# Down weights of experts 3 to 15 asked for by ScalarE instead of SyncE

## The reference, cut to what matters

```python
def _expert_choice_ffn(u, w_router, w_g, w_u, w_d):
    b, n, _ = u.shape
    cap = CAPACITY_FACTOR * n // N_EXPERTS
    logits = jnp.einsum('bnd,de->ben', u, w_router, preferred_element_type=jnp.float32)
    aff = jax.nn.softmax(logits, axis=1)
    gate, idx = lax.top_k(aff, cap)
    bidx = jnp.arange(b)[:, None, None]
    xe = u[bidx, idx]
    hg = jnp.einsum('becd,edf->becf', xe, w_g)
    hu = jnp.einsum('becd,edf->becf', xe, w_u)
    ye = jnp.einsum('becf,efd->becd', jax.nn.silu(hg) * hu, w_d) * gate[..., None].astype(u.dtype)
    return jnp.zeros_like(u).at[bidx, idx].add(ye)
```

## Time and profile before

| | |
|---|---|
| median of 3 runs | 2314.52 us (2312.52 to 2320.67) |
| profiled execution, its time | 2317.68 us |
| profiled execution, its span | 2315.9 us |
| PE busy | 2015.6 us (87%) |
| ACT busy | 541.9 us (23%) |
| DVE busy | 1118.0 us (48%) |
| queue q1, SyncE's (hardware_dynamic): bytes | 737.33 MB |
| queue q0, GpSimd's (software_dynamic): bytes | 19.00 MB |
| queue q10, ScalarE's (hardware_dynamic): bytes | 0.13 MB |
| mean granted TensorE clock | 0.969 |

### The profile page before, as it was taken

How to read it: one execution, slowest core, us unless ns; L and a number is a source line. 1 busy time by engine, 2 the same in 40 slices (tenths; PEclk the granted TensorE clock), 3 DMA queues, 4 the chain that set the end, 5 groups by cost and what they waited for, 6 DMA issues and landing times.

```text
span 2315.9 us, 34904 instructions
## 1 busy us (share of the span) xinstructions
PE 2015.6 (87%) x13636; PEld 1379.1 (60%) x13636; DVE 1118.0 (48%) x1731; ACT 541.9 (23%) x838; POOL 71.6 (3%) x109
## 2 busy tenths in 40 slices
PE   7999999999999999999999986666679998666665
PEld 5999556999899845799886542222239753222222
DVE  3877777878877777887743211000017421100001
ACT  3333133433433223333423100000004210000001
POOL 0000000000000000000300000000000000000000
PEclk9999999999999999999999999999999999899988
DMA  9987876988689777788763899999998699999997
GB/s 347 334 295 261 314 255 214 294 311 302 226 286 322 253 292 255 232 308 313 251 246 104 352 419 421 422 422 422 422 408 281 259 394 421 421 422 422 422 422 317
DMA packets 240449, 757.58 MB, mean 327 GB/s; under 512 B 14016, under 2 KB 124256, under 8 KB 193136
## 3 DMA queue, kind: packets, MB, share of 16 engines
q1 hardware_dynamic: 233248, 737.33, 83.2%
q0 software_dynamic: 6864, 19.00, 2.6%
q10 hardware_dynamic: 256, 0.13, 0.0%
HBM read 755.22 MB, written 1.18 MB: 327 GB/s over the span
## 4 chain that ended last, share of the span: by engine, by line
PE 57%; DMA 32%; DVE 4%; SPq 3%; ACT 1%; issue 1%; DVEq 1%; ACTq 0%
DMA W<-in_w_exp_down 29%; PE psum L870 22%; PE psum L882 10%; PE psum L944 5%; PE psum L925 4%; PE psum L1412 3%; PE psum L1343 2%; SPq L592 2%; PE psum L1150 1%; PE psum L1302 1%; DMA W<-in_w_exp_up 1%; PE psum L787 1%; DMA W<-in_w_conv_in 1%; DMA W_mod<-in_mod_w 1%; PE psum L1324 1%
## 5 line engine op out<-in xcount | busy, mean ns | idle before, releaser
L870 PEld LDWEIGHTS psum<-parts 128*128 128x128 f32 x4224 | 517.8, 192 | 9.1 <-issue 1.9
L870 PE MATMUL psum<-parts 128*128 128x256 f32 x4224 | 521.1, 283 | 1.1 <-ACT parts L1448 0.8
L1302 PE MATMUL psum<-W,scr 128*32 128x512 f32 x1920 | 270.4, 687 | 165.6 <-DMA W<-in_w_exp_up 165.6
L1800 DVE SCALAR_TENSOR_TENSOR mod_acc<-W_mod,cond,mod_acc 128x1024 f32<-128x1024 f32 x196 | 251.8, 1285 | 45.0 <-issue 27.5
L2356 DVE TENSOR_TENSOR scr<-scr,psum 128x256 f32<-128x256 f32 x32 | 13.5, 422 | 530.5 <-ACT scr L1716 530.5
L882 PE MATMUL psum<-parts 128*128 128x512 f32 x1056 | 258.0, 393 | 0.2 <-DVE parts L1995 0.2
L1969 DVE TENSOR_TENSOR parts<-W,parts 128x1024 fp32r<-128x1024 f32 x176 | 207.2, 1220 | 70.2 <-ACT parts L1504 70.1
L1302 PEld LDWEIGHTS psum<-W,scr 128*32 128x32 f32 x1920 | 58.6, 117 | 305.3 <-issue 177.1
L882 PEld LDWEIGHTS psum<-parts 128*128 128x128 f32 x1056 | 192.5, 188 | 45.8 <-DVE parts L1982 7.8
L787 PE MATMUL psum<-k_ones,k_ident 128*128 128x256 f32 x736 | 206.2, 413 | 0.0
L787 PEld LDWEIGHTS psum<-k_ones,k_ident 128*128 128x128 f32 x736 | 135.0, 199 | 103.1 <-issue 89.7
(11 more groups left out here) (329 smaller groups left out, 1700.1 us busy)
## 6 DMA issues: line engine op xcount, KB each, us to landing
W<-in_w_exp_down SPq DMA_DIRECT2D x128, 1024.0 KB, 26.5
W_mod<-in_mod_w SPq DMA_DIRECT2D x123, 1024.0 KB, 6.5
W<-in_w_exp_up SPq DMA_DIRECT2D x120, 1024.0 KB, 26.3
W<-in_w_exp_gate SPq DMA_DIRECT2D x120, 1024.0 KB, 24.9
W<-in_ffn_w_gate SPq DMA_DIRECT2D x44, 1024.0 KB, 9.1
W<-in_ffn_w_up SPq DMA_DIRECT2D x44, 1024.0 KB, 11.6
W<-in_ffn_w_down SPq DMA_DIRECT2D x44, 1024.0 KB, 10.4
W<-in_w_in SPq DMA_DIRECT2D x24, 1024.0 KB, 8.6
```

The costliest lines, as they stand in the source:

```text
L870: ins = pe.matmul(psum[:, 4 + t % 2, S * g:S * g + S], w[:, t % 2, g, kc, :], u[:, kc, :], start=(n == 0 and kc == 0), stop=(n == 2 and kc ...
L1302: ins = pe.matmul(psum[32 * q:32 * q + 32, 4, :].rearrange("p (g n) -> p g n", g=2), x, w[:, :, q, :], start=(b == 0), stop=(b == KC - 1), ...
L1800: ins = dve.scalar_tensor_tensor(acc[:, :], w, col, acc[:, :], mul, add)
```

## The change

The 13 x 4 down blocks of experts 3 to 15, in each of the two layers, are no longer asked for in SyncE's loop. ScalarE asks for them through its own queue, in a new function `down_blocks`, called ahead of the silu of the same expert. The waits are the same ones (d0 to d3 of expert e-1), the source, slot and landing semaphore too.

```diff
--- before.py
+++ after.py
@@ -631,8 +631,6 @@
                 with sp.Fori(3, EXPERTS) as e:
                     for pair in range(4):
                         ring_blocks(layer, e, pair, 2 * pair + 1, e + (E0 - 1))
-                    for q in range(4):
-                        ring_down(layer, e, q, e + (E0 - 1))
 
             def m2_done(name):
                 return m2_pe.s, m2_pe.at(name)
@@ -1725,6 +1723,12 @@
                     act.activation(xeT[:, kc, SOME:512], psum[:, LATE_BANKS[kc % 2], 0:512 - SOME], copy, bias=u_shift[:, kc:kc + 1],
                                    scale=u_scale[:, kc:kc + 1]).then_inc(r_act.sig(f"c{kc}"), 1)
 
+                def down_blocks(e):
+                    for q in range(4):
+                        act.wait_ge(e_pe.s, e_pe.at(f"d{q}", e + (EXPERTS * layer - 1)))
+                        act.dma_start(part(W[:, KC + q, :], 0, 2, D), A["w_exp_down"][layer, ds(e, 1), 256 * q:256 * q + 256, :]
+                                      .rearrange("a (p k) n -> p (a k) n", k=2)).then_inc(landed[KC + q], 16)
+
                 def hidden_out(E):
                     act.wait_ge(e_pe.s, e_pe.at("hT", E))
                     act.activation(e_hT[:, :, :], part(psum[:, 5, :], 0, 4, P)[:, 0:2, :], copy).then_inc(e_act.sig("hT"), 1)
@@ -1737,12 +1741,14 @@
                 hidden_out(EXPERTS * layer + 1)
                 silu(EXPERTS * layer + 2)
                 hidden_out(EXPERTS * layer + 2)
+                down_blocks(3)
                 silu(EXPERTS * layer + 3)
                 for kc in (0, 2, 4, 6):
                     late_out(kc)
                 hidden_out(EXPERTS * layer + 3)
                 with act.Fori(4, EXPERTS) as e:
                     E = e + EXPERTS * layer
+                    down_blocks(e)
                     silu(E)
                     hidden_out(E)
                 roots_next()
```

## The result

The changed kernel takes 2334.1 us (median of 5 runs, 2330.97 to 2337.07), the kernel before 2319.38 us in the 5 runs taken by then (2312.52 to 2324.18). The ratio is 1.0076, 95% interval 1.0057 to 1.0094: slower by about 17 us by the ratio (the two medians lie 14.7 us apart). I had forecast slower by 10.7 us (a ratio of 1.0046) and a range of 2314 to 2333.5. The way was right, the size was too small, and the time lies just outside the range; that the kernel before came out at 2319 and not at 2314.5 in the longer series has a part in the latter.

A forecast was written before the change was run, and what follows sets the result against it. Expert stretches were taken as bound by bytes, so only the order of landing mattered: tails of 7.9 us in layer 1 and 2.8 in layer 0 sum to 10.7, and 2314.5 + 10.7 = 2325.2 us; range 2314 to 2333.5.

The forecast's parts named there:

- The steady stretch: Experts 4 to 15 of either layer: same 12 blocks per period, 29.8 us at 422 GB/s, nothing gained or lost.
- Requests: 104 requests moved from SyncE to ScalarE: cost nothing on both sides, covered by ScalarE's idle time.
- The order of landing: With two queues served in equal turns, the fourth pair's block lands last instead of a down block.
- The tail of 10.6 us: Behind layer 1's last byte: 3.87 us to the first down matmul, 4.4 us of down blocks, 2.3 us to the norm.
- The cover in layer 0: End of layer 0: the square already waited behind the third convolution block's rounding, so only +2.8 us is lost.
- Rival C: Both queues served in the order of asking, blocks land as before: no change, 2314.5 us; chance 0.08.
- D: Two queues cost bytes per us in the expert stretches: 3.5 to 7 us, 2329 to 2332; chance 0.10.
- E: Faster: SyncE's stalls gone, better filled queues move more bytes, each 1% giving 7 us; chance 0.06.
- Rival B: ScalarE's queue gets a third of the turns, fourth down block lands last: about +5.5 us, 2320; chance 0.14.
- Then the queues take turns: Within one expert's period: from 5 us, 4 down and 4 gate or up blocks take 19.9 us, to 24.9.
- The clock term: Each layer's tail: TensorE waits ahead of the third pair, reads it slowly, so the fourth starts 0.7 us late.
- The start costs nothing: At experts 3 and 4, the queues do not run empty, with a margin of 4 us; cost nothing.

The follow-up runs named there:

- experts 6 to 14: Against the kernel before, ScalarE asks for the down blocks of experts 6 to 14 only, SyncE for those of 3 to 5 and 15; ratio 0.9998.
- the run with 8 unread matmuls: Changed kernel with 12 instead of 2 unread matmuls ahead of the third pair, 8 instead of 2 ahead of the fourth; ratio 1.0057 to the kernel before.
- The run that has the start but not the end: Changed kernel with expert 15's four down blocks asked for by SyncE again, in both layers; ratio 1.0023 to the kernel before.

## Why the prediction was short

**Right, by its own steps.** The steady stretch gives and takes nothing (422 GB/s, and 0.9998 for experts 6 to 14). Requests cost nothing that can be seen, on either engine. The second queue isn't served behind the first, and the turns are equal: down blocks land 5.0 us apart. The order of landing changes, the last wait is for an up block, and the loss stands behind it: moving the last expert alone brings most of it, moving it back takes most of it away. The tail of 10.6 us without the clock was right to the tenth in the two traces with a fast fourth pair. The cover in layer 0 was real and is now shown by two runs. Rival C (landing in the order of asking) and D (a lower rate) are excluded by the traces, E by the ratio. Rival B (a third of the turns) had the last wait on a down block and would have them land 7.5 us apart; the last wait was for an up block, and they land 5.0 us apart.

**The step that failed.** "The down slots are free at about 5 ... Then the queues take turns ... to 24.9" lets the turns begin with the request. In the changed kernel the first down block of a group landed 9.0 us after its request, where two turns take 5.0: the turns began about 4 us late. The requests came later too where the fourth pair was read slowly: 7.9 us after the start of that read (2279.59 to 2287.51), not 5. So the eight shared turns reached to the end of the period, the fourth pair landed inside them and not behind them, and it was read 9.85 us after the third instead of 5. The earlier trace rows had a hint of it: GpSimd's first transfer landed 8.6 us after its request, while the second took only 3.7 us behind the first. I had used these rows for the order and the share, not for the start. Two terms of the sum were too small by it.

*The clock term, 0.7 us in each layer.* "24.9 + 3.6 + 2.1 = 30.6" put the fourth pair 5 us behind the third, so that TensorE would be busy in between and fast again. The long wait was to stand ahead of the third pair; there was none in front of it, and TensorE idled for 6.86 us ahead of the fourth and read that in 3.64 us, 1.7 us longer than the 1.93 of a fast one; in layer 0 in 3.28 us, 1.4 longer. The clock of that pair is shown as the cause by the run with 8 unread matmuls. That the slow reads keep each other up isn't the cause of the gap: with a fast read before, and requests at 5.1 us, the third and fourth pair were still 8.9 and 8.2 us apart.

*"The start costs nothing", margin 4 us.* Behind expert 3 the rate sank to 383 and 406 GB/s in two windows of 10 us in layer 0: (39 + 16)/422 x 10 = 1.3 us, and to 325 GB/s for 8 us in layer 1: 1.8 us. The run that has the start but not the end lost 1.6 and 1.8 us in the two stretches. The fourth pair of expert 3 came when the prediction had it: the down matmuls of expert 2 began 4.0 us earlier in this trace (1338.18 against 1342.20), and the pair was read at 1363.50, 4.0 us before the forecast 1367.5. But it was read in 3.64 us instead of 1.92, which shortened the margin. SyncE's last block of expert 4 landed 15.8 us after its request at 1367.76, at 1383.6, and ScalarE's first request for expert 4 stands at 1380.92: 2.7 us were left. The first of its blocks landed 5.2 us after its request, at 1386.1, and the rate sank just between:

```profile
1380.00:1382.00 2.00, 2.00 (x44) 1.20 (x40) 0.00 (x0) 0.00 (x0) 0.00 (x0) 1.00 0.97 344
1382.00:1384.00 2.00, 2.00 (x29) 0.72 (x18) 0.00 (x0) 0.00 (x0) 0.00 (x0) 1.00 0.77 295
```

A margin counted from request to the end of the other queue must hold the time from request to first bytes as well, and it didn't. The smaller dip behind it (406) wasn't followed up.

**The sum by the changed kernel's trace.** From the start of each stretch, the last wait for an expert's block ended 1.1 us later than before in layer 0 and 0.8 us in layer 1 (less than the start's 1.8 there, since the last up block lands 1.5 us ahead of the last byte). Behind it stand 3.8 us more than before in layer 0 and 8.9 in layer 1, where 2.8 and 7.9 were forecast; the difference is mostly the clock. Together 14.6 us where 10.7 were forecast; 15.6 in the second trace of the change.

**Open.** The ratios, 1.0076 and 1.0073, are 17 us of 2316, with intervals from 12 to 22. Whether the 1 to 3 us above the two stretches are chance or belong to the change, these runs don't settle. Nor do they show what passes in the 4 us between a request and its queue's first turn.

## What to carry to other kernels

Where a stretch is bound by bytes, moving requests to another queue changes neither rate nor period, but it changes the order in which the bytes land, because the two queues here were served in turns. Work out what lands last and what stands behind it at the end of each such stretch, and whether the queues can run empty where it begins, and count some microseconds from a request to the queue's first turn (about 4 here). If a stream has to be split, split it so that both queues follow the order of reading. And look at an engine's program for a wait on a late block ahead of work that doesn't need it: that, and not the change, was where about 6 us were to be had.

## What the runs showed of the hardware

Two hardware queues shared the 16 DMA engines at full rate: 422 GB/s with one queue, with a third of the blocks (4 of 12) in the second, and with half of them in it. With 8 KB rows in both, each queue got equal turns: the down blocks of expert 15 land from 9.0 us after the first request on, 5.0 us apart while both queues have work, twice the 2.5 us of a block alone.

TensorE's clock differed from execution to execution in a place that no kernel here touched, the router ahead of the experts. Windows of the kernel before and then of the changed kernel, each over the router of layer 0 and of layer 1 (PEclk is the third number from the end):

```profile
1268.00:1278.00 10.00, 9.57 (x44) 8.91 (x45) 3.62 (x10) 5.19 (x13) 0.00 (x0) 0.60 0.96 397
...
1845.00:1857.00 12.00, 11.25 (x68) 9.47 (x68) 6.77 (x20) 6.08 (x18) 0.00 (x0) 1.00 0.98 391
```

```profile
1268.00:1278.00 10.00, 9.26 (x59) 7.45 (x58) 5.43 (x14) 6.39 (x18) 0.00 (x0) 1.00 0.83 323
...
1845.00:1857.00 12.00, 11.37 (x54) 10.38 (x53) 4.98 (x12) 5.88 (x15) 0.00 (x0) 0.64 0.89 350
```

Each of these two traces has the clock down in one of the two places, and not the same; in the changed kernel with the norm ahead of the rounding it was up in both (1.00 and 1.00). From the first matmul of the convolution to the first down matmul of layer 1 it took 128.3 us with the clock up (1747.29 to 1875.58) and 133.8 with it down (1748.43 to 1882.27); the other traces lie between 128.3 and 133.9. That is 5 us of a kernel's spread, a third of what the change costs, and the reason why the comparison above is made over stretches. What decides it these runs don't tell.
